# The decoder step's start: page table first, block 0 in two halves, four places for turned K

## The reference

```python
z = rmsnorm(x) @ w_in                      # 1024 -> 3584: rq rk rv rg mq mk mv, 512 columns each
ret_o = retention_chunked(rotary(rq), rotary(rk), rv, state, chunk)       # 4 heads of 128
# MoBA, 8 heads of 64: past keys and values come through the page table
k_past = cache_k[pages].reshape(past_len, 8, 64);  v_past = cache_v[pages]...
gate = q . mean(k of each block of 256 keys);  keep the best 3 past blocks and the own one
moba_o = softmax(q k^T / 8, masked to the kept blocks) @ v
hres = x + concat(norm(ret_o) * silu(rg), moba_o) @ w_out
logits = rmsnorm(hres) @ router_w + router_b;  top 4 of 32 experts, softmax weights
u = t @ w_gate_up[e] + b;  a = clamped_swiglu(u);  y += g_e * (a @ w_down[e] + b_down[e])
out = rmsnorm(hres + y)
```

## Time and profile before

| what | value |
|---|---|
| median of 3 runs | 1238.06 us (1237.89 to 1240.36) |
| profiled execution, span from first to last instruction | 1237.4 us |
| the same execution, mean granted TensorE clock | 0.991 |
| moved by DMA | 500.64 MB, mean 405 GB/s |
| DVE turning K units (line 1582) | 32 times, 121.2 us in all |
| MATMUL busy time | 1197.3 us of the span |

### The profile page before, as it was taken

The page is one execution under the profiler, slowest core; times in us unless marked ns, Lnnn a source line. Parts: engine busy times, 40 slices in busy tenths (PEclk is TensorE's granted clock), DMA queues, the critical chain, the costliest instruction groups (busy, mean ns, idle before and its releaser), DMA issues.

```text
span 1237.4 us, 17275 instructions
## 1 busy us (share of the span) xinstructions
PE 1197.3 (97%) x7264; PEld 508.4 (41%) x7264; DVE 382.1 (31%) x555; ACT 239.5 (19%) x560; POOL 68.3 (6%) x70
## 2 busy tenths in 40 slices
PE   6999999999999999999999999999999999999997
PEld 3455544635443434344343434344343434343432
DVE  4999955434311111221111111122111111111122
ACT  4021144504111101121111101021111111110103
POOL 2222202230000000000000000000000000000000
PEclk9999999999999999999999999999999999999999
DMA  8999889999899999999999999999999999999995
GB/s 335 384 361 363 331 331 383 365 384 389 365 421 427 428 427 427 431 427 430 427 430 429 427 431 426 431 427 430 428 427 430 427 430 427 429 429 427 428 427 209
DMA packets 49978, 500.64 MB, mean 405 GB/s; under 512 B 5656, under 2 KB 6320, under 8 KB 19088
## 3 DMA queue, kind: packets, MB, share of 16 engines
q1 hardware_dynamic: 42416, 430.56, 83.2%
q0 software_dynamic: 7520, 69.47, 14.2%
HBM read 495.29 MB, written 4.72 MB: 404 GB/s over the span
## 4 chain that ended last, share of the span: by engine, by line
PE 66%; DMA 21%; DVE 7%; issue 4%; ACT 2%; SPq 0%; DVEq 0%; ACTq 0%
PE psum L1028 24%; DMA arena<-w_gate_up 18%; PE psum L1059 14%; DVE arena L1582 6%; PE psum L936 6%; DMA arena<-w_down 3%; PE psum L956 3%; PE psum L534 3%; PE psum L942 2%; PE psum L754 2%; PE psum L968 2%; PE psum L625 2%; PE psum L454 2%; PE psum L975 1%; PE psum L1095 1%
## 5 line engine op out<-in xcount | busy, mean ns | idle before, releaser
L1028 PE MATMUL psum<-arena 128*64 128x512 f32 x1920 | 421.7, 594 | 11.6 <-DMA arena<-w_gate_up 11.5
L1028 PEld LDWEIGHTS psum<-arena 128*64 128x64 f32 x1920 | 135.0, 137 | 294.6 <-issue 267.8
L1931 DVE TENSOR_SCALAR arena<-psum 128x512 f32<-128x512 f32 x32 | 22.2, 692 | 675.1 <-PE psum L1028 635.7
L1059 PE MATMUL psum<-arena 128*64 128x512 f32 x960 | 212.6, 595 | 0.0
L1185 ACT ACTIVATE arena<-psum 128x512 f32<-128x512 f32 (+3 forms) x190 | 96.2, 509 | 350.3 <-PE psum L1059 170.7
L1582 DVE STREAM_TRANSPOSE arena<-arena 128x2048 f32<-128x2048 f32 x32 | 121.2, 3940 | 2.0 <-PE psum L519 1.9
L1059 PEld LDWEIGHTS psum<-arena 128*64 128x64 f32 x960 | 66.2, 137 | 124.3 <-issue 122.5
L534 PE MATMUL psum<-arena 128*128 128x512 f32 x224 | 107.3, 616 | 0.4 <-ACT arena L1185 0.4
L1455 ACT ACTIVATE arena<-arena 128x512 f32<-128x512 f32 x30 | 18.9, 631 | 412.4 <-DVE arena L1931 412.4
L1185 ACT ACTIVATE arena<-psum,arena 128x128 f32<-128x128 f32 (+2 forms) x162 | 49.1, 401 | 173.6 <-PE psum L534 113.4
L936 PE MATMUL psum<-arena 128*128 128x128 f32 x512 | 76.9, 293 | 0.2 <-DVE arena L1843 0.2
(11 more groups left out here) (264 smaller groups left out, 712.1 us busy)
## 6 DMA issues: line engine op xcount, KB each, us to landing
arena<-w_gate_up SPq DMA_DIRECT2D x128, 2048.0 KB, 31.0
arena<-w_down SPq DMA_DIRECT2D x63, 2048.0 KB, 32.9
arena<-w_in SPq DMA_DIRECT2D x7, 2048.0 KB, 18.4
arena<-w_out SPq DMA_DIRECT2D x2, 2048.0 KB, 12.9
out<-arena POOLq DMA_DIRECT2D x1, 2048.0 KB, 19.8
arena<-w_down SPq DMA_DIRECT2D x2, 1024.0 KB, 38.8
out<-arena SPq DMA_DIRECT2D x3, 512.0 KB, 3.3
arena<-x_prompt SPq DMA_DIRECT2D x2, 512.0 KB, 5.4
```

The costliest lines, as they stand in the source:

```text
L1028: last = mm(psum[64 * g:64 * (g + 1), b, :], xt[:, 2 * kk + m, lhs], gate_slot[slot][:, m, c:c + 512], start=False, stop=kk == 3 and m == ...
L1059: last = mm(psum[64 * g:64 * (g + 1), 2, :], at_sb[:, m, SLOTS * q:SLOTS * (q + 1)], down_slot[slot][:, m, 512 * g:512 * (g + 1)], start=q ...
```

## The change

It has these parts.

- **The page table first.** SP issues it ahead of all else; the four gain loads go to ACT's queue. DVE works out `k_rows` before it evacuates the gains. ACT does a Sqrt on an unused cell before its first real work. DVE works out the V row numbers (lines 1591 to 1594 of before) before the first K unit instead of between the queries' transpose and their copies.
- **Block 0 in two row halves**, with a semaphore for each. PE starts the block's first matmuls on the first half.
- **The prompt's tile ahead of q.** `prompt_part(0, 0)` comes ahead of `sample_part(0)`; on ACT their evacuations change places too. Three of the four pairs of `stay_awake` matmuls go or move.
- **POOL holds K unit 2** (and those behind it) until all of block 0 has landed. SP issues block 2 ahead of the constants' tail.
- **DVE turns two K units ahead of the queries' work** instead of one, and the 32 copies of the queries become 16.
- **Four places for turned K**: two of before and two in words 12288 to 16383, which nothing else uses then. Unit u waits for the scores of unit u-4. V set 2, which uses the same words, now waits until all units are scored.
- **K units in pairs** at places given by `K_AT`, the last pair in `prompt_part(5, 0)` instead of the last unit in `prompt_part(4, 1)`. ACT's evacuations of the scores are put to match.

```diff
+        KT_AT = (DN, DN + 2048, 12288, 14336)
+        def kt_sb(u):
+            return at(KT_AT[u % 4], 4 * 512)
...
-        UNITS_IN = (3, 3, 3, 3, 3, 4, 3, 3, 4, 3, 0, 0, 0, 0)
+        K_AT = {(0, 1): (5,), (1, 0): (2, 7), (1, 1): (5,), (2, 0): (1, 5), (2, 1): (2, 7), (3, 0): (1, 7),
+                (3, 1): (4,), (4, 0): (0, 6), (4, 1): (4,), (5, 0): (1, 6)}
...
             for tile in range(2):
-                stay_awake(5, 2)
                 pe.wait_ge(x_in[tile], 16)
...
-            stay_awake(5, 2)
             pe.wait_ge(x_scaled, 1)
             n_x = transposes(A, [x_sb[0:NS, 2, k * P:(k + 1) * P] for k in range(KC)], NS)
+            stay_awake(5, 2)
...
+                if tile == 0:
+                    pe.wait_ge(*((win_in[b % 3], 16 * (b // 3 + 1)) if b else (block0_half, 16)))
...
                 for k in range(KC):
+                    if b == 0 and tile == 0 and k == 4:
+                        pe.wait_ge(win_in[0], 16)
...
-                    for u in range(first + units * k // KC, first + units * (k + 1) // KC):
-                        k_unit(u)
+                    if k in K_AT.get((b, tile), ()):
+                        k_unit(units_done[0])
+                        k_unit(units_done[0] + 1)
+                        units_done[0] += 2
...
+            prompt_part(0, 0)
             q_bank = A.bank()
-            stay_awake(5, 2)
             mark["q_sample"] = (a_full, sample_part(0), q_bank)
-            prompt_part(0, 0)
             mq = prompt_part(0, 1)
...
+            act.dma_start(gain_in[0:8, :], t["norm1_g"][0].rearrange("(k p) -> k p", p=P)).then_inc(gains_in, 16)
...
             act.wait_ge(zeroed, 1)
+            nc.scalar.activation(stat[:, 63:64], stat[:, 62:63], ACT.Sqrt)
...
+                    if u >= 4:
+                        dve.wait_ge(k_scored, u - 3)
-                    if u >= 2:
-                        dve.wait_ge(k_scored, u - 1)
...
-                    for u in range(2):
-                        dst = qk[32 * s:32 * (s + 1), :, 4 * c + 2 * u:4 * c + 2 * u + 2,
-                                 16 * u + s:16 * (u + 1):4]
-                        ins = v.tensor_copy(dst, src[:, s, u])
+                    ins = v.tensor_copy(qk_heads(c)[32 * s:32 * (s + 1), :, :, :, s:16:4], src[:, s])
...
             for u in range(K_UNITS):
+                if u == 2:
+                    pool.wait_ge(win_in[0], 16)
...
-                elif n > 2:
+                elif n == 2:
+                    pool.wait_ge(k_scored, K_UNITS)
+                else:
                     pool.wait_ge(v_used, n - 2)
...
+            sp.dma_start(page_all, t["page_table"].rearrange("s n -> (s n)").partition_broadcast(P)).then_inc(pages_in, 16)
             sp.dma_start(consts[:, 0:head], t["shape_consts"][:, 0:head]).then_inc(consts_in, 16)
...
-            load_block(0)
+            first = w_in[:, :, 512 * BLOCKS[0]:512 * (BLOCKS[0] + 1)]
+            sp.dma_start(win[:, 0, 0:4], first[:, 0:4]).then_inc(block0_half, 16)
+            sp.dma_start(win[:, 0, 4:8], first[:, 4:8]).then_inc(win_in[0], 16)
             load_block(1)
+            load_block(2)
             sp.dma_start(consts[:, head:], t["shape_consts"][:, head:ncols]).then_inc(tables_in, 16)
-            load_block(2)
```

More of the change, by code:

```diff
@@ L239, in build_kernel, with qk_heads @@
         k_raw = at(KV, 4, 4 * 512)
+        def kt_sb(u):
+            return at(KT_AT[u % 4], 4 * 512)
+        def qk_heads(c):
+            both = at(Q + 2304 + 128 * c, 2, 512)[:, :, 0:160].rearrange("p g (u r) -> p g u r", u=2)
+            return both[:, :, :, 0:64].rearrange("p g u (w x) -> p g u w x", w=2)
         HT = cur; cur += 2304
@@ L437, in build_kernel @@
         V_SETS = PAGES
-        UNITS_IN = (3, 3, 3, 3, 3, 4, 3, 3, 4, 3, 0, 0, 0, 0)
-        assert sum(UNITS_IN) == K_UNITS
+        K_AT = {(0, 1): (5,), (1, 0): (2, 7), (1, 1): (5,), (2, 0): (1, 5), (2, 1): (2, 7), (3, 0): (1, 7),
+                (3, 1): (4,), (4, 0): (0, 6), (4, 1): (4,), (5, 0): (1, 6)}
+        assert 2 * sum(map(len, K_AT.values())) == K_UNITS
         @block.tensor
@@ L522, in k_unit @@
                 last.then_inc(k_scored, 1)
+            units_done = [0]
             def prompt_part(b, tile, amid=None):
[L526 to L529, removed]
+                if tile == 0:
+                    pe.wait_ge(*((win_in[b % 3], 16 * (b // 3 + 1)) if b else (block0_half, 16)))
                 w = win[:, b % 3]
@@ L1299, in _ @@
             ins.then_inc(q_own_ready, 1)
+            evacuate_scores(2)
             evacuate_block(z[:, 2])
@@ L1556, in evacuate_t @@
                                         psum[:, V.bank(), 0:4 * w].rearrange("p (c w) -> p c w", c=4)))
-            evacuate(gain, width=28)
+            dve.wait_ge(consts_in, 16)
             dve.wait_ge(pages_in, 16)
@@ L1565, in _ @@
             ins.then_inc(k_rows_ready, 1)
+            evacuate(gain, width=28)
             dve.wait_ge(x_rms, 1)
@@ L1570, in _, with k_transposes @@
             evacuate_scaled(h_t, P, 1, range(4, 8), gain)
+            link(v.tensor_tensor(v_pages, page_all.rearrange("p (n m) -> p n m", m=8),
+                                 const("page").unsqueeze(1).broadcast_to([P, 2 * SEQS, 8]), ALU.mult))
+            link(v.reduce_sum(v_first, v_pages, axis=AXX))
+            v.tensor_scalar(v_rows, v_first, const("lane")[:, 1:2], None, ALU.add).then_inc(v_rows_ready, 1)
+            def k_transposes(first, last):
+                for u in range(first, last):
+                    dve.wait_ge(k_in[u % 4], 16 * (u // 4 + 1))
+                    if u >= 4:
+                        dve.wait_ge(k_scored, u - 3)
+                    v.transpose(kt_sb(u).rearrange("p (e b r) -> p r e b", e=16, b=32),
+                                k_raw[:, u % 4, :]).then_inc(k_trans, 1)
+            k_transposes(0, 1)
             dve.wait_ge(x_rms, 2)
@@ L1574, in _ @@
             dve.wait_ge(zeroed, 2)
-            def k_transposes(first, last):
-                for u in range(first, last):
-                    dve.wait_ge(k_in[u % 4], 16 * (u // 4 + 1))
-                    if u >= 2:
-                        dve.wait_ge(k_scored, u - 1)
-                    v.transpose(kt_sb[:, u % 2, :].rearrange("p (e b r) -> p r e b", e=16, b=32),
-                                k_raw[:, u % 4, :]).then_inc(k_trans, 1)
-            k_transposes(0, 1)
+            k_transposes(1, 2)
             q_full, q_n, q_bank = mark["q_sample"]
```

32 lines of the change are left out of this document (11 added, 21 removed).

## The result

The changed kernel takes 1246.19 us in the median of 4 runs (1245.51 to 1249.72), beside 1238.53 us for the kernel before (1237.89 to 1240.36): the ratio is 1.0064, with a 95% interval of 1.0051 to 1.0076. It is slower by 7.7 us, where 14 us less was forecast. The profiled execution has a span of 1244.7 us and took 1246.51 us.

What follows compares the result with a forecast made beforehand. The experts' weight stream bounds the kernel, starting only after a 315 us front where DVE leads. 8.4 + 1.9 - 1.3 + 5.9 = 14.9, less 0.9, leaves 14 us: 1224 us, range 1218 to 1234.

Steps and rivals of the forecast that it cites:

- Edits at nothing: Start of the kernel: gain loads, early Sqrt, V row numbers and removed `stay_awake` matmuls counted as 0 us.
- whatever the 315 us in front of it lose, the whole kernel loses: Experts' weight stream of 379 MB can't be shortened and starts at 314.70 us, so only an earlier start gains.
- block 0 late: Rival, start: block 0 lands behind the gathers; at 36 us the kernel is 3 us slower, 1241; 1 in 20.
- given back: Rival, up to the experts: DMA near full share keeps only 2 to 4 us, 1234 to 1236; 1 in 12.
- the lower clock in block 0's first tile: Bound, start: PE at half clock, second half takes 6.9 us for 3.4, third turn at 28.5; no chance given.
- The third K unit: Start of the K units: DVE's third turn begins at 25.1 us instead of 33.5, 8.4 us earlier.
- the bound of 19.2: Start: block 0 landing at 19.2 us instead of 17, which leaves the third turn 6.2 us earlier.
- Four places: K units: DVE's one wait for PE's scores goes, 1.9 us gained, between 0 and 1.9.
- Contention: K units: weight blocks queued beside K's transfers cost 1.3 us, between 0 and 5.
- Half share: Rival, K units: K gets half the bandwidth while weights are queued; gain 11 us, 7 with slow clock; 1 in 5.
- The order at the end: End of K units: second group of turned probabilities 14.0 us after the last turn instead of 19.9, 5.9 us gained.
- Downstream: From 168.8 to 314.7 us: same work shifts as it is, less 0.9 us for transfers following closer.

Runs made afterwards that it cites:

- the last experiment: Changed kernel plus six tiny matmuls whose result is unread, block 0's sample matmuls between the two halves of the prompt's tile: 1223.38 us, ratio 0.9880.
- the units alone: Kernel before with only four places for turned K, units in pairs, V set 2's later wait and ACT's order to match: 1230.08 us, ratio 0.9924.
- With the loop in place: Changed kernel plus six tiny matmuls, result unread, ahead of block 0's second half, so the experts' loop stands where it stood before: 1224.42 us, ratio 0.9887.
- -24: The changed kernel itself, its experts' loop starting 24 PE instructions ahead of the old place: 1246.19 us.
- +232: Changed kernel plus 64 small unread matmuls ahead of block 0's second half, loop 232 instructions behind the old place: 1244.74 us in one run.

## Why the prediction was wrong

**The step that failed** is the line under "Edits at nothing", "The removed `stay_awake` matmuls filled waits", with the opening's "whatever the 315 us in front of it lose, the whole kernel loses". I asked of the six matmuls what they cover in time, and of the experts only when their stream starts; I took the loop as unmoved because its code and its order are. Their work was indeed worth nothing. Their 24 instructions were not: without them the loop stands where each jump back fetches it anew, and PE loses 10 us on each of four, 41 us. The weights standing ready in the nine places, and PE's waits for them that fell away, took up part of it, and 22.0 us reached the end. The waits of PE for w_gate_up (us, times, longest) show some of that part, of the kernel before:

```profile
PE psum L1028 <- DMA arena<-w_gate_up: 11.5, 16, 1.2
```

The changed kernel has none of them, and the one of before with twelve idle matmuls has half:

```profile
PE psum L1034 <- DMA arena<-w_gate_up: 6.4, 8, 1.2
```

Why it isn't less than 22: three pairs are 75 MB (six experts of 12 MB), an estimate of 177 us at the 427 GB/s of the earlier trace rows, and PE takes 168 us for them without a pause and 178 with one. Without a pause PE uses up what stood ready and then keeps to the stream; with it, PE is the slower of the two from start to end, and the chain is 93% PE. The rounds of the loop bear this out. From the first matmul of one round to that of the next the timeline has 168.0, 168.0, 168.0, 175.2 and 176.2 us before, and 170.3, 178.6, 178.4, 178.0 and 177.2 after; from the last pair's first matmul to the end it is 68.3 and 63.4. So four rounds lost, and the stretches that the stream had bounded before gave some of it back. By that account pauses of 2 us, 170 to 174 us for three pairs, would cost nothing, and yet they cost 7 us; that rest stays open.

None of the rivals had this. The one with the other sign, block 0 late, didn't occur: PE waited 2.37 us for its second half, until 18.59. The gain wasn't given back either, since the experts began at 299.99 us, and the lower clock in block 0's first tile didn't come: its last 8 records took 3.70 us.

**The front, term by term** (choice and later points of the kernel after against the earlier trace rows):

- *The third K unit, forecast 8.4 us earlier, measured 33.5 - 29.16 = 4.3.* The path was right, the size off by half. The first gather went out at 6.26 us, not 5: the constants' head, now second in SP's queue, landed at 4.2; that cost nothing, as the first two turns were done before the queries. Block 0 was there at 18.6, not 17, close to the bound of 19.2. The sample took 3.2 us, from 22.22 to 25.5, for 1.95. The 16 copies took 3.22 us, 0.20 each, for 2.1: 1.1 more, just over the "0 to 1 us" that the doubled elements might cost, which I had named and set at nothing.
- *Four places, forecast 1.9: held.* No wait for PE is left in the row of line 1598, and the choice starts at 142.43, 6.2 us earlier, which is 4.3 + 1.9.
- *Contention, forecast -1.3: measured 0.* After the first unit DVE never waits for K, with all DMA engines busy. Half share, a rival at 1 in 5, is refuted. Only where the queries came earlier still did landings count, 4.1 us in the last experiment.
- *The order at the end, forecast 5.9: measured 6.2.* The second group of turned probabilities comes at 156.45 for 168.81, 12.4 us earlier, less the 6.2 above. The exponentials follow the choice, but the table load, which I had put between the two, lies inside the choice (147.21 to 148.49 us), and at the end ACT waits 0.86 us for the sample's matmuls of PE. My terms for this side add up to 14.3 us and not to the 14.0 that I wrote; 14.0 is what was measured (142.43 to 156.45), so the agreement is partly luck. The kernel with the units alone shows 6.3.
- *Downstream, forecast -0.9: measured +2.3.* From 156.45 to 299.99 us it is 143.5, and 145.9 before. The two windows below, of before and then of after, show one place of it: at nearly the same time PE's clock was 0.50 in the one and 1.00 in the other, and 36 transposes took 6.26 us in the first. That state comes and goes between kernels with the same order there: the kernel before with twelve idle matmuls has 1.00 in this window. Its own stretch from these probabilities to the experts is 142.1 us for the 145.9 of the kernel before, so this term scatters by more than the 2.3 us, which I don't count as the change's doing.

```profile
216.00:220.00 4.00, 4.00 (x22) 1.92 (x18) 1.91 (x2) 0.60 (x1) 0.00 (x0) 0.50 1.07 405
```

```profile
216.00:220.00 4.00, 4.00 (x43) 2.75 (x41) 1.82 (x7) 2.25 (x3) 2.95 (x2) 1.00 1.06 424
```

The sum in front is 4.3 + 1.9 + 0 + 6.2 + 2.3 = 14.7, what was measured, against 14 forecast, so errors of both signs cancelled (4.1 us too much at the third unit; 1.3, 0.3 and 3.2 too little behind it). That the front came out near 14 is luck in part. With the loop in place the kernel takes 1224.4 us, and 1224 was predicted; that doesn't make the prediction right, since the kernel that was asked about doesn't have its loop in place. One small reading of mine was off: PE had no work from 24.42 us on, and not from 24.2.

**What I could have seen.** The page of before has 32 packets in the instruction queue, and the order of the two programs shows fewer PE instructions ahead of a real loop. The kernel has a function `place_loop` in `prompt_part`, whose name says what it is about, and I passed over it. What it asks for, nops, isn't in the built program of either kernel, so it isn't what keeps the loop in its place.

## What to carry to other kernels

Where an engine has a real loop and little time to spare in it, every instruction added or removed ahead of it moves the loop and can cost what happened here: compare the instruction queue's packets of the two profiles first, and look for pauses put down to issue at the jumps back. A front's gain is to be read at the start of the long stage, and the long stage by its own length, since a total of +7.7 us hid -14.7 and +22.0. And an early start pays only as far as the buffers behind it let it: with two places for turned K 1.3 us of it reached the choice, with four 4.3.

## What the runs showed of the hardware

- The jump back of this loop of 1,747 PE instructions shows no pause in some places and a whole refetch, 9 packets of 16 KB, in others, with a period of 256 instructions. The loop is shorter than the 2,048 that the Trainium skill, "Runtime: NRT & Kernel Launch", section "Instruction fetch mechanics", gives for PE's instruction memory, so being shorter wasn't enough here.
- One refetch, under a full weight stream, stopped PE for about 2 us (1.8 to 2.5), and in the two places -24 and +232 for about 5 more (4.7 to 5.2) after one further record. After the two pauses the clock was at 0.50 for about 5 us, which made 16.0 us of 13.9.
- An idle matmul of 128 by 8 columns took 0.114 us per record in the kernel before (24 in 2.74 us), one with 8 columns of weights too 0.026 us in the changed kernel (128 records in 3.35 us): with two records per matmul, 24 instructions can be had for 1.4 or for 0.3 us.
